# RG-LRU recurrence of an encoder layer: gelu projections one place ahead of their gates in the second half, and a gates' slab asked for ahead of the wait for remainder scans

## What is computed

```python
u_lru, g_lru, q, k, v, gate_lru, gate_attn = jnp.split(x @ w_in + b_in, SPLIT_IDX, axis=-1)
u = depthwise_conv(u_lru, w_lru_conv, b_lru_conv, LRU_CONV_PAD)
# per direction (forward, backward), block-diagonal weights of 160 x 160
r = sigmoid(block_diag_linear(u, w_a, b_a)); i = sigmoid(block_diag_linear(u, w_x, b_x))
log_a = 8 * r * log_sigmoid(lam);  a = exp(log_a)
bt = sqrt(-expm1(2 * log_a)) * (i * u)
h = scan(h = a * h + bt)            # along the positions
y_lru = ((h_fwd + h_bwd) * gelu(g_lru)) @ w_lru_out
```

## Time and profile before

| | us |
|---|---|
| median of 3 runs | 2766.47 |
| lowest, highest | 2766.07, 2767.06 |
| profiled execution, its own time | 2770.9 |
| its span, first to last instruction | 2769.1 |
| TensorE matmul busy | 2671.8 (96%) |
| VectorE busy | 1506.4 (54%) |
| ScalarE busy | 753.4 (27%) |
| GpSimd busy | 654.1 (24%) |
| granted TensorE clock, mean | 0.985 |

### The profile page before, as it was taken

One profiled execution on the slowest core, in us unless ns is written; L12 is line 12 of the kernel. 1 busy time (PEld: TensorE's weight loads), 2 busy tenths in 40 slices (PEclk: granted clock), 3 DMA queues, 4 the chain that ended last, 5 costly groups with the idle time before them and its releaser, 6 DMA issues.

```text
span 2769.1 us, 32046 instructions
## 1 busy us (share of the span) xinstructions
PE 2671.8 (96%) x11898; PEld 2202.5 (80%) x11898; DVE 1506.4 (54%) x1800; ACT 753.4 (27%) x1033; POOL 654.1 (24%) x332
## 2 busy tenths in 40 slices
PE   8997999999899999999999999989999999999998
PEld 6886788888678877888888888878788778888886
DVE  7899864334313657745445464667742314644445
ACT  4565713313210022010101011148831211211112
POOL 3554531231133612334343433310000000000000
PEclk9998999999899999999999999999999999999999
DMA  6565654444686833434343534357756794544554
GB/s 232 183 204 185 213 193 160 172 157 159 262 353 231 301 125 137 137 137 153 136 179 128 188 124 161 132 215 235 244 186 228 256 343 159 205 183 182 192 201 168
DMA packets 174272, 535.67 MB, mean 193 GB/s; under 512 B 13863, under 2 KB 40743, under 8 KB 172112
## 3 DMA queue, kind: packets, MB, share of 16 engines
q1 hardware_dynamic: 116992, 430.94, 43.1%
q10 hardware_dynamic: 57168, 103.21, 10.5%
HBM read 310.99 MB, written 214.19 MB: 190 GB/s over the span
## 4 chain that ended last, share of the span: by engine, by line
PE 82%; DVE 9%; DMA 4%; ACT 2%; issue 1%; POOL 1%; ACTq 0%; SPq 0%; DVEq 0%; POOLq 0%
PE ps L857 48%; PE ps L1176 12%; PE ps L1003 8%; PE ps L1097 4%; PE ps L907 3%; PE ps L1036 2%; PE ps L986 2%; DMA gate_in<-gate_dram 1%; DMA W<-w_split 1%; PE ps L1023 1%; PE ps L910 1%; PE ps L1165 1%; DVE tau L1750 1%; DMA al_dram<-AOL 0%; DMA w_split<-W 0%
## 5 line engine op out<-in xcount | busy, mean ns | idle before, releaser
L857 PE MATMUL ps<-XH,W 128*128 128x512 f32 x4224 | 1208.2, 392 | 24.9 <-DVE XL L1695 11.6
L857 PEld LDWEIGHTS ps<-XH,W 128*128 128x128 f32 x4224 | 798.0, 189 | 202.1 <-issue 18.4
L857 PE MATMUL ps<-XL,W 128*128 128x512 f32 x2112 | 712.1, 391 | 0.0
L857 PEld LDWEIGHTS ps<-XL,W 128*128 128x128 f32 x2112 | 399.2, 189 | 83.1
L1176 PE MATMUL ps<-W,HH 128*128 128x512 f32 x1152 | 310.4, 389 | 1.7 <-DVE HL L2006 1.5
L1176 PEld LDWEIGHTS ps<-W,HH 128*128 128x128 f32 x1152 | 216.1, 188 | 47.3 <-DVE HL L2006 1.9
L741 POOL TENSOR_SCALAR W<-raw 128x1024 fp32r<-128x1024 f32 (+2 forms) x72 | 95.4, 1325 | 587.2 <-PE ps L857 277.6
L1003 PE MATMUL ps<-XH,W 128*128 128x512 f32 x672 | 216.4, 393 | 0.0
L807 POOL TENSOR_SCALAR W<-raw 128x1024 fp32r<-128x1024 f32 x72 | 87.4, 1213 | 535.3 <-PE ps L857 224.9
L742 POOL TENSOR_TENSOR W<-raw,W 128x1024 fp32r<-128x1024 f32 (+2 forms) x72 | 200.5, 2785 | 6.0
L808 POOL TENSOR_TENSOR W<-raw,W 128x1024 fp32r<-128x1024 f32 x72 | 191.9, 2666 | 6.0
(11 more groups left out here) (203 smaller groups left out, 3360.6 us busy)
## 6 DMA issues: line engine op xcount, KB each, us to landing
w_split<-W SPq DMA_DIRECT2D x131, 1024.0 KB, 6.4
W<-w_split SPq DMA_DIRECT2D x130, 1024.0 KB, 6.9
raw<-w_mlp SPq DMA_DIRECT2D x72, 512.0 KB, 4.9
raw<-w_qkv_mix SPq DMA_DIRECT2D x28, 512.0 KB, 3.9
w_split<-W SPq DMA_DIRECT2D x8, 1280.0 KB, 12.0
W<-w_split SPq DMA_DIRECT2D x8, 1280.0 KB, 7.7
gate_dram<-mix_out ACTq DMA_DIRECT2D x16, 512.0 KB, 2.7
gate_in<-gate_dram ACTq DMA_DIRECT2D x16, 512.0 KB, 6.2
```

Source lines behind the costliest of these rows:

```text
L857: last = nc.tensor.matmul(bank(group, c), lhs(wl, k), rhs(xl, k, c), start=(k == 0 and n == 0), stop=(k == nk - 1 and n == 2))
```

## The change

It does four things.

1. In the second half g11, g12 and g13 stand ahead of gates11, gates12 and gates13. The order is now gates10, g10, u12, g11, gates11, u13, g12, gates12, gR1, g13, gates13, for both sequences.
2. ScalarE's list of what it takes after a block's roots is written out (`taken_behind`). It takes g10 inside the decays of block 10, between the squares of its two directions, and no longer after its roots. All other takes stay where they were.
3. For sequence 0, in both halves, SyncE issues a gates' load ahead of the moves of the block before. At jj = 1 the save of the slab two back also comes ahead of the wait for scans and of the moves into `sigr`.
4. For sequence 1 a `gates` step at jj = 1 does what it did (stack, wait for scans, move); with the new order g11's slab is fetched ahead of it.

```diff
-                     ("gates", 1, 0), ("g", 1, 0), ("u", 1, 2),
-                     ("gates", 1, 1), ("g", 1, 1), ("u", 1, 3),
-                     ("gates", 1, 2), ("g", 1, 2), ("g", 1, REST_TILE),
-                     ("gates", 1, 3), ("g", 1, 3)]
+                     ("gates", 1, 0), ("g", 1, 0), ("u", 1, 2), ("g", 1, 1),
+                     ("gates", 1, 1), ("u", 1, 3), ("g", 1, 2),
+                     ("gates", 1, 2), ("g", 1, REST_TILE), ("g", 1, 3),
+                     ("gates", 1, 3)]
+        taken_behind = {(0, 0): (("g", 0, 0), ("u", 0, 2), ("g", 0, REST_TILE)), (0, 1): (("g", 0, 1), ("u", 0, 3)),
+                        (0, 2): (("g", 0, 2), ("u", 1, 0)), (1, 0): (("u", 1, 2),),
+                        (1, 1): (("g", 1, 1), ("u", 1, 3)), (1, 2): (("g", 1, 2), ("g", 1, REST_TILE))}
...
+                def stack_second(q, T, h):
+
+                    sp.wait_ge(slab_done, first_slab(q, "lru") + slab_at[("gates", h, 0)] + 3)
+                    stack_rests(sp, q, T, h, 1)
+
                 def moves_of_block(q, T, h, jj):
 
-                    if jj == 0:
-                        sp.wait_ge(slab_done, first_slab(q, "lru") + slab_at[("gates", h, jj)] + 3)
-                        stack_rests(sp, q, T, h, jj + 1)
-                        if h:
-                            sp.wait_ge(scan_done[q], 2 * REST_TILE + 4)
+                    if h and jj == 0:
+                        sp.wait_ge(scan_done[q], 2 * REST_TILE + 4)
                     move_rest_gates(sp, q, T, h, jj)
...
-                    if kind == "gates" and jj:
-                        moves_of_block(0, T, h, jj - 1)
                     if kind == "gates":
                         load(n, n % 2, A["w_gate"][HALF * h + jj, :, :], GATEW)
                         sp.dma_start(gs_raw[:, :], A["w_gate_rest"][HALF * h + jj, :, :]).then_inc(stack_in, 16)
                     else:
                         load(n, n % 2, A["w_" + kind][feature_tile(h, jj), :, :])
+                    if kind == "gates" and jj > 1:
+                        moves_of_block(0, T, h, jj - 1)
+                    if kind == "gates" and jj == 1:
+                        stack_second(0, T, h)
                     if n == 2:
                         sp.wait_ge(x_landed[KD // 2 - 1], 16)
                     if n >= 2:
...
+                    if kind == "gates" and jj == 1:
+                        moves_of_block(0, T, h, 0)
...
+                        if jj == 1:
+                            stack_second(1, T, h)
                         if jj:
                             moves_of_block(1, T, h, jj - 1)
...
-                    def decays(h, jj, r):
+                    def decays(h, jj, r, between=lambda: None):
...
                             act.wait_ge(decay_done[q], 6 * n + d + 3)
+                            if d:
+                                between()
...
-                            decays(h, jj, [side(r, jj, T) for r in sig[0:2]])
+                            decays(h, jj, [side(r, jj, T) for r in sig[0:2]],
+                                   (lambda: take("g", 1, 0)) if (h, jj) == (1, 0) else (lambda: None))
...
-                                for e in behind_gates(h, jj):
+                                for e in taken_behind[h, jj]:
                                     take(*e)
```

More of the change, by code:

```diff
@@ L509, in feature_tile @@
             return BLOCKS + h if jj == REST_TILE else HALF * h + jj
-        def behind_gates(h, jj):
-            at = slab_at[("gates", h, jj)] + 1
-            out = []
-            while at < len(order_lru) and order_lru[at][0] != "gates":
-                out.append(order_lru[at])
-                at += 1
-            return out
         phases = ["lru", "attn", "mlp"]
```

## The result

The changed kernel takes 2794.76 us, the median of 4 runs (2792.47 to 2800.5), beside 2766.76 for the kernel before on the same chip (2766.07 to 2767.79): a ratio of 1.0103, 95% interval 1.0091 to 1.0116. It is 28.0 us slower, where 15.1 were forecast, and it lies above the range.

A forecast was written before the change was run, and what follows sets the result against it. TensorE, busy 96% of the span, was taken as the bound, with 19.4 us of waits for GpSimd's gates slab. First sequence +2.7 and second +12.4 made +15.1 on the 2766.5 median: 2781.6 us, range 2770 to 2788.

The forecast's parts named there:

- The 15.02 us wait goes: Second half, T=1024: TensorE's 15.02 us idle before gates11, waiting for GpSimd's split of its slab, disappears.
- the four of 1.1: T=1024: the 1.1 us waits before gates02, gates03, gates12 and gates13 go; the first half's two give -2.2.
- I cost that at nothing; the cover is some 2 us: First half, T=1024: later moves into `sigr` delay block 00's gelu some 5 us, still ready before gR0; cost nothing.
- They come 2.2 earlier, at 244.2: Second half, T=1024: block 10's scans end at 244.2, not 246.43, leaving a 5.1 gap inside gates11, ending at 253.7.
- The chain behind gates11, T=1024: g12, g13 and m=1 wait for gelus, gaps 1.8, 3.8 and 6.6; 120.5 to the first transpose against 119.5, +1.0.
- T=512: Second sequence, second half: gates11's end +1.3, the gelu-bound chain behind it +7.5, clock +3.6, sum +12.4 us.
- +1.3: Second half, T=512: gates11 ends at 1961.8 against 1960.51, g11 having waited for g10's gelu with a 1.4 gap.
- The clock: TensorE's granted clock drops behind the gaps before g13 and m=1, 1.8 each: +3.6 in each sequence.
- Rival A: The losses of clock don't come, or lie under waits: about +6, total 2772; chance 0.11.
- I pass these on in full: Phases after the recurrence start from TensorE, so the sequences' delays reach the total undiminished: +15.1 us.
- Rival C: More is lost: GpSimd later by 3 costs 3, short gaps lose clock too; +20, 2787; chance 0.10.
- Rival D: TensorE's own slot holds gates11's split until u12 ends; without g11 in front, a gap of 10. Counted in C.

The follow-up runs named there:

- narrow_splits: The changed kernel with GpSimd's splits of g11's and gates11's slabs cut to 128 of their 1024 and 640 columns; 2796.5 us, one run.
- gelu_early3: gelu_early with SyncE's whole old list at jj = 1 in both halves; 2762.0 us, ratio 0.9982 to the kernel before.
- fetch_after_store: gelu_early3 where, at T=512, SyncE fetches gates11's slab only after a y store has landed; 2759.8 us, ratio 0.9977 to the kernel before.
- g11_only: The changed kernel with g12 and g13 back behind their gates, only g11 ahead; 2771.9 us, ratio 1.0020 to the kernel before.
- sp_only: The kernel before with only SyncE's part of the change, order and ScalarE's list as before; 2769.3 us, ratio 1.0007 to the kernel before.
- split_after_scans: fetch_after_store with GpSimd's split of g11's slab, first sequence, begun only after the remainder's scans; 2764.6 us, ratio 0.9984 to the kernel before.
- gelu_early2: gelu_early with the first half's moves into sigr put back ahead of the save; 2764.4 us, ratio 0.9991 to the kernel before.
- order_only: The changed kernel with SyncE's list as before, keeping the new order and ScalarE's takes; 2791.3 us, ratio 1.0085 to the kernel before.
- gelu_early: The changed kernel with the gelus of g11, g12 and g13 taken earlier by ScalarE; 2768.5 us, ratio 1.0004 to the kernel before.

## Why the prediction was wrong, step by step

- **The 15.02 us wait goes**: right, and so do the four of 1.1. **"I cost that at nothing; the cover is some 2 us"**: wrong by 1.29, gR0's wait. The first half brought about 1.2 and not 2.2.
- **"They come 2.2 earlier, at 244.2"** is the step that failed most. It let VectorE keep its instruction lengths while GpSimd was moved beside them; the sentence after it even gave GpSimd's new place as a gain of 0 to 1.5. The scans ended at 250.9. The wait inside gates11 was 10.75 and not 5.1, and gates11 ended at 260.7 (where u13's first product starts) and not at 253.7: **+7.0** on the forecast. Of the 6.7 at the scans 1.0 is the first half, and 5.7 are VectorE's lengths, as added up above. narrow_splits took 3.8 off by cutting the splits of two slabs. What it left is mainly the 2.8 beside u13's split, which it had not touched and which lands on a scan there. Beside it, a slip in the sum: 244.2 + 2.4 is 246.6, not 246.8.
- **The chain behind gates11, T=1024**: right in its places and sizes. Gaps of 3.54, 3.51 and 6.35 stand for 1.8, 3.8 and 6.6, 1.2 more in all.
- **T=512**: "+1.3" for gates11's end was some +3.2: its wait for g10's gelu was 2.65 and not 1.4, since the y store landed late behind fetches that the new order placed there (shown on gelu_early3 by fetch_after_store). The chain's gaps, 1.50, 2.88, 4.69 and 7.48, make 16.6 where 17.5 were forecast.
- **The clock**: charged at 1.8 for two gaps in each sequence, 3.6. What is left of the two chains when their gaps are taken out is 5.1 us more, in both, than the same instructions in the forecast. g12's gap at T=1024 lost it too (0.50 in the row above), and behind gaps near 2.6 us it is either. Rival A, that these losses don't come, falls: behind the gaps before g13 and m=1 the clock was 0.50 and 0.70 at T=1024, 0.50 and 0.64 at T=512. The price of 1.8 itself came from one execution's 0.64 behind 1.99 us; behind the same gap g11_only has 1.00 (1.98), sp_only 0.64 (1.97). The Trainium skill, "TensorE: Matmul & The Clock Gate", section "Why this matters for your kernels", asks for no long idle gaps between bursts of matmuls and would let these pass; the row behind 2.65 agrees, those behind 2.56 and 1.99 do not.
- **The sum**: 7.0 + 1.2 + 1.5 in the first sequence and 1.9 - 0.9 + 1.5 in the second are 12.2 us over the forecast's 15.1, which makes 27.3; the two lengths gave 27.2.
- **"I pass these on in full"**: right for the loss (27.2 in the lengths, 28.0 in the medians). For the gains it was about half: fetch_after_store is 12.0 shorter in the lengths and 7.2 in the median. Why the rest gives 2 to 5 us back there was not settled. A part can be read: all runs with the early gelus have a wait of 1.1 to 1.3 us for VectorE's `VL` shortly behind the second sequence's first transposes, and the kernel before has none.
- **Rival C** named GpSimd's lateness as its mechanism; what decided was VectorE's, caused by an early GpSimd. **Rival D**: in the changed kernel TensorE's slot did hold the split, to 228.35, and g11 covered it. For the early load alone it was wrong: in sp_only the slab takes the slot that g10's had, GpSimd splits it from 217.25, and gates11 starts with 1.79 us idle; what is left is the 16.7 for block 10's scans, and not a gap of 10 for GpSimd.

## What to carry to other kernels

A wait that is removed may hide another of the same length for another engine: the prediction followed the next releaser of the same step (here the scans, 2 us behind the slab), but not what the freed engine would now run beside. When GpSimd work is moved, look at which VectorE instructions it lands on and add its length to them. A later split of gates11's slab was worth more here than an early one; a later split of g11's was not (split_after_scans). And where a step in PSUM's turn needs an activation, take it as early in ScalarE's list as its buffer allows: the order that cost 28 us became 7 us faster than the kernel before by moving three gelus, one SyncE list and one fetch.

## What was not expected of the hardware

- The same 128x1024 scan takes 2.29 us alone and up to 4.38 beside GpSimd's splits, and GpSimd's head copy of a 128x1024 slab takes 3.14 where it starts together with a scan; in the kernel before the same copy took from 1.04 to 2.76.
- Behind one and the same idle time of TensorE, 2.52 to 2.65 us before g11 at T=512, the granted clock over the next 4.7 us was 1.00 in two executions (changed, gelu_early2) and 0.64 to 0.66 in five (order_only, g11_only, narrow_splits, gelu_early, gelu_early3).
- A y store of 2 x 256 KB at T=512 was waited for 4.4 us after its issue with a DMA share of 0.86, and 2.8 us with 0.67.
